# A mixer layer's latent keys: the shared rotary rows turned once, ahead of the head norms

## What is computed

```
k_rope = broadcast(k_rope_raw[:, :, None, :], (b, s, 8, 32))
k = concatenate([k_nope, k_rope], axis=-1)          # 96 per head
k = rms_norm(k, kh_g)                               # one factor per head and token, one gain per channel
k = concatenate([k[..., :64], apply_rope(k[..., 64:], cos, sin)], axis=-1)
```

## Time and profile before

| what | value |
|---|---|
| median of 3 runs | 2118.43 us (2117.85 to 2120.16) |
| span of the profiled execution | 2122.4 us |
| TensorE matmul busy | 2027.5 us, 96% |
| VectorE busy | 911.2 us, 43% |
| ScalarE busy | 644.2 us, 30% |
| chain that ended last: TensorE's share | 71% |

### The profile page before, as it was taken

The page is one execution under the profiler, slowest core; times in us unless marked ns, Lnnn a source line. Parts: engine busy times, 40 slices in busy tenths (PEclk is TensorE's granted clock), DMA queues, the critical chain, the costliest instruction groups (busy, mean ns, idle before and its releaser), DMA issues.

```text
span 2122.4 us, 32004 instructions
## 1 busy us (share of the span) xinstructions
PE 2027.5 (96%) x12406; PEld 1304.4 (61%) x12407; DVE 911.2 (43%) x1611; ACT 644.2 (30%) x981; POOL 56.2 (3%) x65
## 2 busy tenths in 40 slices
PE   6999999999999999999999999999999999999999
PEld 4864333433333323332343498979999999799999
DVE  2522122112222112221122365866885558776774
ACT  1422111111111111110111234553554354634653
POOL 0000000000000000000000121000000120000000
PEclk9997999999999999999999999999999999999999
DMA  9785999299999999999769953413665544234563
GB/s 347 276 325 243 412 417 417 118 417 417 419 418 417 417 419 418 417 417 418 287 257 418 366 159 117 157 64 100 199 214 164 164 140 145 82 120 159 172 196 110
DMA packets 222041, 580.37 MB, mean 273 GB/s; under 512 B 23520, under 2 KB 142048, under 8 KB 185984
## 3 DMA queue, kind: packets, MB, share of 16 engines
q1 hardware_dynamic: 221952, 579.09, 71.7%
HBM read 577.74 MB, written 1.31 MB: 273 GB/s over the span
## 4 chain that ended last, share of the span: by engine, by line
PE 71%; DMA 12%; SPq 8%; DVE 4%; ACT 3%; issue 2%; ACTq 0%; DVEq 0%
PE bank L1085 13%; DMA ring<-in_w_gu 9%; PE bank L1141 8%; SPq L685 4%; PE bank L1229 3%; SPq L687 3%; PE bank L812 3%; PE bank L1231 3%; PE bank L1230 3%; PE bank L1462 3%; PE bank L1464 3%; PE bank L1463 3%; PE bank L1037 3%; PE bank L1051 3%; PE bank L882 2%
## 5 line engine op out<-in xcount | busy, mean ns | idle before, releaser
L1085 PE MATMUL bank<-ring,heap 128*64 128x512 f32 x2176 | 491.6, 600 | 31.1 <-DMA ring<-in_w_gu 31.1
L1085 PEld LDWEIGHTS bank<-ring,heap 128*64 128x64 f32 x2176 | 148.3, 137 | 357.4 <-issue 262.7
L2091 DVE TENSOR_SCALAR heap<-bank 128x256 f32<-128x256 f32 (+1 forms) x72 | 26.7, 413 | 724.0 <-PE bank L1085 695.2
L1141 PE MATMUL bank<-ring,heap 128*64 128x512 f32 (+1 forms) x1152 | 255.1, 595 | 0.0
L1229 PE MATMUL bank<-h_hi,w_hi 128*128 128x256 f32 x640 | 185.7, 290 | 1.2 <-DVE w_lo L2177 1.2
L2372 DVE TENSOR_TENSOR w_lo<-ring,w_hi 128x2048 fp32r<-128x2048 f32 (+1 forms) x64 | 142.4, 2225 | 101.3 <-ACT w_hi L1785 101.3
L1462 PE MATMUL bank<-h_hi,w_hi 128*128 128x256 f32 x640 | 182.3, 285 | 3.4 <-DVE w_lo L2372 3.4
L1613 ACT ACT_TABLE_LOAD x32 | 41.1, 1283 | 470.3 <-DVE heap L2091 468.6
L1230 PE MATMUL bank<-h_lo,w_hi 128*128 128x256 f32 x640 | 182.8, 286 | 0.0
L1231 PE MATMUL bank<-h_hi,w_lo 128*128 128x256 f32 x640 | 182.8, 286 | 0.0
L1464 PE MATMUL bank<-h_hi,w_lo 128*128 128x256 f32 x640 | 181.8, 284 | 0.0
(11 more groups left out here) (350 smaller groups left out, 2987.4 us busy)
## 6 DMA issues: line engine op xcount, KB each, us to landing
ring<-in_w_gu SPq DMA_DIRECT2D x256, 1024.0 KB, 19.2
ring<-in_w_down SPq DMA_DIRECT2D x128, 1024.0 KB, 21.7
ring<-in_ffn_w_up SPq DMA_DIRECT2D x44, 1024.0 KB, 7.7
ring<-in_w_in SPq DMA_DIRECT2D x32, 1024.0 KB, 7.9
ring<-in_w_ada SPq DMA_DIRECT2D x24, 1024.0 KB, 10.5
ring<-in_ffn_w_down SPq DMA_DIRECT2D x16, 1024.0 KB, 5.2
ring<-in_w_out SPq DMA_DIRECT2D x8, 1024.0 KB, 5.0
ring<-in_w_in SPq DMA_DIRECT2D x3, 2048.0 KB, 26.7
```

The costliest lines, as they stand in the source:

```text
L1085: last = mm(psum[g][both[f], :], xgT[:, k % 4, k // 4, :], wt[:, g, :, :, f, :].rearrange("p i c n -> p (i c) n"), start=False, stop=k == ...
L1141: last = mm(psum[2][FEW * f:FEW * f + n, :], hidT[:, o:o + n], wt[:, 512 * f:512 * (f + 1)], start=k == 0, stop=k == DT - 1)
```

## The change

- After the grouped queries are copied out, VectorE multiplies the 32 rotary rows by their gain into a new small tile `k_rope` (signal `kgain`). TensorE multiplies them by the 32 x 32 corner of the swap matrix in a new fill `swkr`, between `ssgk` and gates 0. VectorE sets the gain of channels 64 to 95 to 1, and after unit 6 forms the sine product, the cosine product and the sum on 32 x 256 (signal `krope`).
- ScalarE squares the unrotated rotary rows (broadcast over 4 heads) and the plain rows into two tiles `k_sq`, which share their place with the later `turned_q`; four activations, ahead of the copies of `uv`. `ssk` reads `k_sq` in place of `L["sq"]`. The copy of the rotary rows to the heads now takes the rotated ones and stands after gates 4.
- The fills `swk0` to `swk3` go (8 matmuls of 96 x 96 by 256 columns), and with them TensorE's wait for the scaled keys between gates 6 and gates 7, and VectorE's four sine products, its cosine product, its sum and a wait. TensorE waits for the scaled keys (`kn`) ahead of the first latent head instead.
- Fills behind `swkr` move by one bank up to gates 6, and by three the other way behind it; the four banks of the down-projection are renumbered.

```diff
-        turned_at = [take(4, T) for _ in range(3)][0:2]
+        turned_at = [take(4, T) for _ in range(2)]
+        k_sq = turned_at
+        turn = take(2, T)
+        k_rope, k_turn = turn[64:96, 0, :], turn[64:96, 1, :]
...
-                 ("ssgk", "dve"), ("ga0", "act"), ("ga1", "act")]
+                 ("ssgk", "dve"), ("swkr", "dve"), ("ga0", "act"), ("ga1", "act")]
...
-        order += [(f"swk{i}", "dve") for i in range(4)] + [("ga7", "act")]
+        order += [("ga7", "act")]
...
-        DOWN_BANKS = (3, 4, 5, 6)
+        DOWN_BANKS = (0, 2, 3, 4)
...
+                done("kgain")
+                mm(lay("swkr")[64:96, 0:T], const("swap_m")[64:96, 64:96], k_rope, start=True, stop=True) \
+                    .then_inc(lay_full.sem, 1)
                 gates(0)
...
-                    squares(f"ssk{i}", const("ones")[0:MQ, 0:MQ], L["sq"], [(2 * i, 1), (2 * i + 1, 1)], MQ)
+                    o = 2 * (i % 2)
+                    squares(f"ssk{i}", const("ones")[0:MQ, 0:MQ], k_sq[i // 2], [(o, 1), (o + 1, 1)], MQ)
...
-                for n in range(3, 7):
+                for n in range(3, 8):
                     gates(n)
-                done("kn")
-                for i in range(4):
-                    tiles_of(lay(f"swk{i}"), const("swap_m")[0:MQ, 0:MQ], L["mk"], 2 * i, MQ).then_inc(lay_full.sem, 1)
-                gates(7)
...
-                            done("rope_m", 3)
+                            done("rope_m", 2)
+                            done("kn")
...
-                f(L["mk"][64:96, :, :], L["krope"][64:96, :].unsqueeze(1).to_broadcast([32, NH, T]), ACT.Copy) \
-                    .then_inc(S["krope"].sem, 1)
+                own("uk3")
+                for i in range(2):
+                    f(k_sq[i][64:96], L["krope"][64:96, :].unsqueeze(1).to_broadcast([32, 4, T]), ACT.Square)
+                    ins = f(k_sq[i][0:HD], L["mk"][0:HD, 4 * i:4 * i + 4, :], ACT.Square)
+                ins.then_inc(S["ksq"].sem, 1)
...
-                ready("krope")
-                own("uk3")
-                f(L["sq"][0:MQ], L["mk"][0:MQ], ACT.Square).then_inc(S["ksq"].sem, 1)
...
                 gates(4)
+                ready("krope")
+                f(L["mk"][64:96, :, :], k_rope.unsqueeze(1).to_broadcast([32, NH, T]), ACT.Copy)
                 ready("kvar", 2)
...
+                v.tensor_scalar(k_rope, L["krope"][64:96, :], v2("k_head", 0)[64:96], None, ALU.mult).then_inc(S["kgain"].sem, 1)
...
                 rest_early(6)
+                ready("kgain")
+                c.mark(v.memset(v2("k_head", 0)[64:96], 1.0))
+                taken(v.tensor_tensor(k_turn, full("swkr")[64:96, 0:T], const("sin_m")[64:96], ALU.mult))
+                c.step(v.tensor_tensor(k_rope, k_rope, const("cos_m")[64:96], ALU.mult))
+                own("swkr")
+                v.tensor_tensor(k_rope, k_rope, k_turn, ALU.add).then_inc(S["krope"].sem, 1)
...
                 ready("kn")
-                turned("k", turned_k)
                 rest_early(12)
-                c.mark(v.tensor_tensor(mk, mk, cos, ALU.mult))
-                c.settle()
-                own("swk3")
-                v.tensor_tensor(mk, mk, L["rs"][0:MQ], ALU.add).then_inc(S["rope_m"].sem, 1)
-                ready("rope_m", 1)
                 ready("qstd")
```

More of the change, by code:

```diff
@@ L54 @@
 STOP = None
-LCH = {"dve": 125, "pool": 23}
+LCH = {"dve": 126, "pool": 23}
 ROUNDS = 4
@@ L539, in build @@
             "gsq": 1, "gvar": 1, "gstd": 1, "gn": 1, "rope_g": 1, "qvar": 1, "qstd": 1,
-            "ksq": 1, "kvar": 2, "kstd": 1, "kn": 1, "rope_m": 3, "krope": 1, "mixed": 1,
+            "ksq": 1, "kvar": 2, "kstd": 1, "kn": 1, "rope_m": 2, "kgain": 1, "krope": 1, "mixed": 1,
             "nmax": 2 * NH, "fold": 2, "pnorm": 2 * NH, "merged": 4, "sq2": 4, "var2": 1, "std2": 1,
@@ L2252, in _ @@
                     taken(v.tensor_tensor(dst, two(full(name)), sin, ALU.mult))
-                mq, mk = L["mq"][0:MQ], L["mk"][0:MQ]
+                mq = L["mq"][0:MQ]
                 turned_q = [x[0:MQ] for x in turned_at]
-                turned_k = [L["rs"][0:MQ, 4 * n:4 * n + 4, :] for n in range(2)]
                 def turned(q, dst):
@@ L2334, in _ @@
                     elif i == 2:
-                        ready("rope_m", 3)
+                        ready("rope_m", 2)
                 out_act("ga11")
```

## The result

| kernel | median | from, to | runs |
|---|---|---|---|
| before | 2120.65 us | 2117.85 to 2126.16 | 10 |
| changed | 2126.49 us | 2122.2 to 2129.66 | 10 |

The ratio is 1.0026, with a 95% interval from 1.0015 to 1.0037: slower by 5.5 us, between 3.2 and 7.8. A second set of runs (the experiment `again`) gave 1.0031 [1.0021, 1.004]. The prediction said 2122.6 and a range up to 2126.0, so the median lies 3.9 us above the one and 0.49 us above the other, outside the range. Two things are mixed in that: the kernel before is now at 2120.65 us, not at the 2118.43 of its first three runs, and the difference is 5.8 us where 4.2 were forecast.

What follows compares the result with a forecast made beforehand. It took TensorE and VectorE as both full, with gates 7 waiting for VectorE's unit 11. To 2118.43 us it added 2 x 0.6 for `swkr` and 2 x 1.5 for clock falls: 2122.6 us, range 2118.0 to 2126.0.

Steps and rivals of the forecast that it cites:

- The 3.60 us of `swk` gain nothing: TensorE ahead of gates 7: removed swap products become a 3.6 us pause, as gates 7 waits for VectorE's unit 11; gain 0.
- Rival (b): Ahead of gates 7: VectorE finishes unit 11 earlier, so TensorE takes the 3.6 us; 2112.4 us if wholly; chance 0.07.
- VectorE's 7 us and all its small additions: VectorE: 7.0 us removed behind unit 11 become idle time; five added operations, under 2.5 us a layer, hide in idle time.
- ScalarE's cover: ScalarE: the keys' root comes 1.9 us later, still 1.6 us before VectorE wants it; cost taken as 0.
- Rival (d): ScalarE's cover is thinner than 1.6 us and the keys' scaling waits for the root; 2124.6 at 1 us a layer; chance 0.05.
- `swkr` at 0.6 us: TensorE ahead of gates 0: the added small product costs 0.6 us a layer, 1.2 in all, bounds 0.9 and 1.5.
- A fall at 1.5 us a layer: Gates 7: the pause pulls TensorE's clock to half, costing 1.5 us in each layer, bounds 0.8 and 3.0.
- Rival (a): At gates 7 the pause leaves the clock alone or pulls it down in one layer only; 2119.6 or 2121.1 us; chance 0.28.
- Rival (c): At gates 7 the falls are longer, two stretches of half rate in each layer; 2125.6 us; chance 0.15.
- The sum: Both layers: 2 x 0.6 for the small product plus 2 x 1.5 for clock falls, 4.2 us over the median, 2122.6.
- The sum is made against: Whole kernel: terms are added to the median of the runs, 2118.43 us, 4.0 us below the profiled span of 2122.4.
- Slower by over 0.2%: Whole kernel: outcome more than 0.2% (4.2 us) slower, chance 0.43, beside 0.50 within 0.2% and 0.07 faster.

Runs made afterwards that it cites:

- again: The changed kernel with nothing altered, run a second time; median 2127.01 us beside 2120.59 us of the kernel before, ratio 1.0031.
- early11: The changed kernel with VectorE's rest of unit 11 moved ahead of the keys' scaling and two cosine products; median 2121.37 us, ratio 1.0004 to before.
- fix: `early11` with ScalarE's copy of the rotated rows ahead of gates 2 and VectorE's scaling of the keys behind unit 12; median 2115.20 us, ratio 0.9972 to before.
- fill8: The changed kernel with 8 products that nobody reads put between gates 6 and gates 7; median 2120.82 us, ratio 0.9999 to before.
- fill4: The changed kernel with 4 products that nobody reads put ahead of gates 7; median 2124.27 us, ratio 1.0017 to before.
- fill4b: A second profile of `fill4`, the changed kernel with 4 unread products ahead of gates 7; that execution took 2121.89 us.

## Why the prediction was right in its mechanism and short in its sum

**The 3.60 us of `swk` gain nothing: right, shown.** The pause is there, with the length and the releaser that were named, and gates 7 follows unit 11 within 0.05 us. When unit 11 moves, the pause moves (`early11`), and when VectorE is early enough the whole 3.60 us appear in the way (`fix`). Rival (b) had this mechanism and its condition right; the change did not meet it.

**VectorE's 7 us and all its small additions are hidden; ScalarE's cover holds: right.** The list up to unit 11 is 37.23 us long, and the root ends 1.6 us ahead of its reader. Rival (d) did not occur.

**`swkr` at 0.6 us: too small.** "I take 0.6" stood on a share of the array's change of shape read from `s_g0`, with 0.77 as the upper bound. It is 0.83 us at gates 0, outside the bounds, and 0.74 us over the way to `s_g0`. For both layers 1.5 us in place of 1.2. The 0.16 us are what `s_g0` costs beyond its columns on 64 rows, both sides together; for 32 rows the same excess was measured at 0.39 us.

**A fall at 1.5 us a layer: right for three of four.** The four measured lengthenings are 2.33, 1.50, 1.51 and 1.50 us, with a mean of 1.71, so 3.4 us in place of 3.0. The Trainium skill, "TensorE: Matmul & The Clock Gate", section "HAM oscillation — how this bites in real kernels", says that bursts with long waits between them lose the clock and start over slow. The trace agrees for the pause of 3.44 us, four times in four. Rival (a), no or one fall, had 0.28 and is refuted; `fill8` takes the pause away and the loss with it. Rival (c), longer falls, had the time nearest to the measured one (2125.6), but not for its reason: one fall of the four was long, and it cost 2.33 us and not 3.0.

**The sum** with the measured terms is 1.5 + 3.4 = 4.9 us, inside the interval of 3.2 to 7.8, with 4.2 forecast. Of the 3.9 us by which the time is above 2122.6, 2.2 are the base, 0.7 are these two terms, and the last 1.0 lies within what the interval leaves open; it is not assigned to a cause.

**The step that failed is the first one**, "The sum is made against": the terms were added to the median of three runs, 2118.43, as if it were exact. With ten runs the kernel before is at 2120.65. With that base the same terms give 2124.9, and a range up to 2128.2 that holds the measured 2126.49. The profiled execution was a sign of it: in the later runs the device time is the span plus about 1.8 us, so the span of 2122.4 was a time of some 2124.2 us, 5.8 above that median. In 23 runs on one chip the kernel before reaches from 2115.39 us, with a mean granted clock of 0.991, to 2126.23 with 0.986; the falls behind `ssq` alone add between 0 and 3 us a layer. The range took in the bounds of the terms and none for the base. Slower by over 0.2% stood at 0.43 beside 0.50 for no change. It came, though the first interval (1.0015 to 1.0037) still reaches below 0.2%; that of `again` (1.0021 to 1.004) doesn't. The forecast of 4.2 us lay on that border, and the terms that were too small kept it there.

## What to carry to other kernels

When two engines are full side by side, work that is taken off the one that waits turns into a pause, unless the other's list ahead of the meeting gets shorter in the same edit; look for that first, and move the freed engine's next piece of weights forward. A pause in dense matmuls can cost more than its own length, so a change that "only" lays a hidden wait bare is not free. In the pause itself, work that nobody reads took most of the loss back (`fill8`), and moving the other engine's work forward turned the loss into a gain (`fix`). Before you forecast a difference of 0.2%, ask how far single executions of the same kernel lie apart, and put that into the range.

## What the hardware showed

- In the two layers the clock fell for 3.41 or 6.83 us at a time. At the pause of 3.44 us of idle time it fell four times in four, for 3.41 us three times and 6.83 us once; behind 1.59 us of idle time (`early11`) and 1.71 (`fill4`), at the same place, not once in eight layers. At the wait in the feed-forward part it fell in 8 layers of 8 with 1.80 to 2.89 us of idle time and in none of 20 with 1.06 to 1.63. A fall costs 1.50 us if it lies wholly over dense matmuls, and the long one 3.03 us behind `ssq`, but 2.33 us where a part of it lay in the pause.
- The same kernel at the same matmuls sometimes has the fall behind `ssq` and sometimes not, and `fill4b` had it some 26 us earlier, at the end of `swkr`. With the falls of the feed-forward part this accounts for a part of the spread between executions; how much was not measured.
- One plain fp32 product on 32 rows between products on 128 (rows 64 to 95) costs 0.39 us beside its columns with 32 columns of weights and 0.44 with 96; on 96 rows that excess isn't there.
